# Two transformer blocks on one core: the first mixture of experts gathers for four experts and spreads for two, with rows over 32 handled in conditions; values of the second attention one step later

## The reference, cut to what matters

```python
logits = xt @ w_router + b_router
top_v, top_e = lax.top_k(logits, TOP_K)          # TOP_K = 4, N_EXPERTS = 32
weights = softmax(top_v)
hcat = x_pad[tok] @ w1[e] + b1[e]                # 1024 -> 2048
x_glu = minimum(hcat[:, ::2], 7.0)
x_lin = clip(hcat[:, 1::2], -7.0, 7.0)
act = x_glu * sigmoid(1.702 * x_glu) * (x_lin + 1.0)
y = act @ w2[e] + b2[e]                          # 1024 -> 1024
out = sum(y[dest] * weights)                     # over the token's 4 experts
```

## Time and profile before

| | us |
|---|---|
| median of 3 runs | 2189.37 |
| lowest, highest | 2186.71, 2189.53 |
| the profiled execution's own time | 2187.02 |
| its span | 2185.2 |
| mean granted TensorE clock | 0.927 of full |

### The profile page before, as it was taken

How to read it: one execution, slowest core, us unless ns; L and a number is a source line. 1 busy time by engine, 2 the same in 40 slices (tenths; PEclk the granted TensorE clock), 3 DMA queues, 4 the chain that set the end, 5 groups by cost and what they waited for, 6 DMA issues and landing times. The chain is left out here.

```text
span 2185.2 us, 28329 instructions
## 1 busy us (share of the span) xinstructions
PE 1818.3 (83%) x11496; PEld 826.7 (38%) x11496; DVE 804.7 (37%) x1613; ACT 506.8 (23%) x1028; POOL 77.5 (4%) x96
## 2 busy tenths in 40 slices
PE   7899998999999998989987797699889855665556
PEld 3655445433333433424333233255544522222221
DVE  2215533333342444434443334588782200000001
ACT  2022302232331233332333233222310200000000
POOL 0000000000000000000000000084000000000000
PEclk9999999999999999989999999799999878887888
DMA  7845359789897799999999999534128299999997
GB/s 281 287 136 191 136 173 388 314 350 409 343 420 312 309 424 423 423 422 399 425 423 423 422 423 423 180 121 178 54 101 345 87 429 427 427 428 428 427 429 322
DMA packets 114820, 713.55 MB, mean 327 GB/s; under 512 B 16799, under 2 KB 21102, under 8 KB 69006
## 3 DMA queue, kind: packets, MB, share of 16 engines
q1 hardware_dynamic: 106208, 704.98, 79.1%
q10 hardware_dynamic: 8398, 5.47, 0.8%
HBM read 709.35 MB, written 1.07 MB: 325 GB/s over the span
## 5 line engine op out<-in xcount | busy, mean ns | idle before, releaser
L881 PE MATMUL ps<-ring,ar 128*32 128x512 f32 x3072 | 371.9, 624 | 44.3 <-DMA ring<-in_w 31.6
L481 PE MATMUL ps<-ar 128*128 128x128 f32 (+5 forms) x1742 | 351.4, 359 | 38.3 <-PEq L755 16.4
L488 PE MATMUL ps<-ring,ar 128*32 128x512 f32 x1184 | 196.1, 692 | 139.0 <-DMA ring<-in_w_gate 49.2
L481 PEld LDWEIGHTS ps<-ar 128*128 128x128 f32 (+2 forms) x1742 | 233.9, 200 | 159.4 <-issue 114.3
L481 PE MATMUL ps<-ring,ar 128*128 128x512 f32 (+2 forms) x592 | 247.0, 577 | 4.9 <-ACT ar L2266 2.6
L881 PEld LDWEIGHTS ps<-ring,ar 128*32 128x32 f32 x3072 | 97.8, 113 | 314.3 <-issue 264.7
L1825 DVE TENSOR_SCALAR ar<-ps 128x256 f32<-128x256 f32 x128 | 54.4, 425 | 409.7 <-PE ps L881 400.9
L893 PE MATMUL ps<-ring,ar 128*32 128x512 f32 x1536 | 173.8, 598 | 0.0
L596 PE MATMUL ps<-ring,ar 128*128 128x512 f32 x384 | 171.9, 599 | 0.0
L481 PEld LDWEIGHTS ps<-ring,ar 128*128 128x128 f32 x592 | 112.4, 191 | 132.8 <-issue 126.2
L2400 ACT ACTIVATE ar<-ps 64x512 f32<-64x512 f32 x256 | 151.5, 592 | 45.1 <-PE ps L893 30.7
(11 more groups left out here) (403 smaller groups left out, 1379.0 us busy)
## 6 DMA issues: line engine op xcount, KB each, us to landing
ring<-in_w SPq DMA_DIRECT2D x192, 2048.0 KB, 20.4
ring<-in_w_gate SPq DMA_DIRECT2D x25, 2048.0 KB, 29.1
ring<-in_w_up SPq DMA_DIRECT2D x25, 2048.0 KB, 31.4
ring<-in_w_down SPq DMA_DIRECT2D x24, 2048.0 KB, 29.8
ring<-in_w_in SPq DMA_DIRECT2D x21, 2048.0 KB, 9.0
ring<-in_w_ada SPq DMA_DIRECT2D x12, 2048.0 KB, 8.3
ar<-in_w_up SPq DMA_DIRECT2D x7, 2048.0 KB, 29.8
ar<-in_w_gate SPq DMA_DIRECT2D x7, 2048.0 KB, 29.3
```

The costliest lines, as they stand in the source:

```text
L481: ins = self.t.e.matmul(o, l, r, start=(i == 0), stop=(i == len(pairs) - 1))
L488: ins = self.t.e.matmul(b[32 * i:32 * i + 32, :], l, r, start=(k == 0), stop=(k == len(steps) - 1))
L881: ins = e.matmul(b[32 * s:32 * s + 32, :], HG[:, 2 * c + r, 32 * n:32 * n + 32], W[:, r, HALF(s)], start=False, stop=(c == 3 and r == 1))
```

## The change

In the first mixture:
- The first 32 rows of four experts are gathered by one set of sixteen matmuls (32 columns each) into `HG4`, during the turn of expert 4g-1. The first four experts are split in two and two (`HEAD = 2`).
- Rows 33 to 128 are gathered for each expert in the condition on 32 rows, in the first half of its first layer, between pass 0 and the further passes, into `HGX` (96 columns). ACT copies them for every expert.
- The weights of the first 32 rows are turned for two experts together, and their spread (`spread_pair`, K = 128) runs once per two experts, during the turn of the even one. The weights of the further rows are turned and copied in the second layer, in the condition on 32.
- The spread of the further rows (`spread_further`) is in the condition on 32 (before: 64), with an inner condition on 96 per token block.
- YV is set to zero at the start and all spreads are added. Activations (`ATB`) and gathered further rows have one buffer instead of two.

In the second attention the values run one step later (15 steps instead of 14).

The second mixture's functions are only renamed. The diff, cut to its core:

```diff
-    HGB = [A(1024 * i, 8, 128) for i in range(2)]
-    ATB = [A(2048 + 1024 * i, 8, 128) for i in range(2)]
+    HG4, HGX, ATB, ACB = A(0, 8, 128), A(1024, 8, 96), A(1792, 8, 128), A(2816, 4, 256)
+    YGP, YGX, YG3 = A(3840, 1024), A(4864, 1024), A(HT, 1024, part=(64, 128))
...
+    HEAD = 2
...
+    def gather_four(t, w, g, lo, n):
+        t.wait_ge(s_dve, dve["pick4", g, lo])
+        t.wait_ge(s_act, act["rows", 1])
+        for h in range(2):
+            b = w.claim("hg", 1, g, lo, h, lane=TL1)
+            for k in range(4):
+                o = b[:, 128 * k + 32 * lo:128 * k + 32 * lo + 32 * n]
+                pe["hg", 1, g, lo, h, k] = w.sums(o, [(XNV[:, tb, TB(4 * h + k)], SB4[:, tb, 32 * lo:32 * lo + 32 * n])
+                                                     for tb in range(2)])
+
+    def turn_pair(t, w, j):
+        b = w.claim("swtp", j, lane=TL1)
+        t.wait_ge(s_dve, dve["selp", j])
+        for tb in range(2):
+            ins = t.e.transpose(b[:, TB(tb)], SWBP[:, tb, :], ident)
+        pe["swtp", j] = t(ins)
...
+    def spread_pair(t, w, j):
+        t.wait_ge(s_act, act["ygp", j])
+        for tb in range(2):
+            for h in range(2):
+                b = w.claim("spp", j, tb, h, lane=TL1)
+                pe["spp", j, tb, h] = w.sums(b[:, :], [(SWTP[:, TB(tb)], YGP[:, HALF(h)])])
...
+        def spread_further(u, count):
+            def further_rows():
+                t.wait_ge(s_act, act["ygx", u])
                 for tb in range(2):
+                    bs = [w.claim("spx", u, tb, h, lane=TL1X) for h in range(2)]
+                    k = z.n
+                    with e.If(count > 96):
...
+                    z.n = k
+                    with e.Else():
+                        for h in range(2):
+                            psp[u, tb, h] = z(e.matmul(bs[h][:, :], SWTX[:, TB(tb)], YGX[:, HALF(h)], start=True,
+                                                       stop=True))
+            either(t, z, count, 32, further_rows)
...
+                def gather_further():
+                    t.wait_ge(s_dve, dve["pickx", u])
+                    for h in range(2):
+                        for k in range(4):
+                            for tb in range(2):
+                                ins = e.matmul(hx[h][:, 96 * k:96 * k + 96], XNV[:, tb, TB(4 * h + k)],
+                                               SBX[u % 2][:, tb, :], start=(tb == 0), stop=(tb == 1))
+                        px["hx", u, h] = x(ins)
...
                 def second():
+                    if half == 0:
+                        gather_further()
+                    t.wait_ge(s_act, act["hx", u, half])
                     only(t, count, 64, third)
                     x(further(1))
...
             if u > 0:
-                spread1(u - 1, counts[u - 1])
+                spread_further(u - 1, counts[u - 1])
+            if u > 0 and u % 2 == 0:
+                spread_pair(t, w, u // 2 - 1)
...
             pe["at", u, 0] = t(turn_act(0, (0,)))
-            if u + 1 < NE:
-                gather(t, w, 1, u + 1, TL1)
+            if u == HEAD - 1:
+                gather_four(t, w, 0, HEAD, 4 - HEAD)
+            elif u % 4 == 3 and u + 1 < NE:
+                gather_four(t, w, u // 4 + 1, 0, 4)
+            if u > 0 and u % 2 == 0:
+                turn_pair(t, w, u // 2)
             turn_act(1, (1,))
+            at2, swx = w.claim("at", u, 2, lane=TL1), w.claim("swx", u, lane=TL1)
...
             with e.If(count > 32):
                 only(t, count, 64, lambda: turn_act(2, (2, 3)))
+                t.wait_ge(s_dve, dve["selx", u])
+                for tb in range(2):
+                    e.transpose(swx[:, TB(tb)], SWBX[:, tb, 0:128], ident)
+                    ins = e.transpose(swx[0:64, TB(2 + tb)], SWBX[:, tb, 128:192], ident)
+                px["swx", u] = x(ins)
...
-        for s in range(14):
+        for s in range(15):
             if s < 12:
                 scores(s)
-            if s >= 2:
+            if 2 <= s < 14:
                 turn_p(t, w, 2, s - 2, (0, 1), 2)
...
-            if s >= 2:
-                values(s - 2)
+            if s >= 3:
+                values(s - 3)
...
         vector_ada(v, 5, 1)
+        v(v.own.memset(YV, 0.0))
...
         for u in range(NE):
+            if u > 0 and u % 2 == 0:
+                vector_selectp(v, u // 2)
+            vector_selectx(v, u)
...
+            if u % 4 == 3 and u + 1 < NE:
+                vector_pick4(v, u // 4 + 1, 0, 4, RKP)
             if u + 1 < NE:
-                vector_pick(v, 1, u + 1)
-                vector_select(v, 1, u + 1)
+                vector_pickx(v, u + 1)
...
                 if n == 0 and u > 0:
-                    vector_spread(v, 1, u - 1)
+                    vector_spread_further(v, u - 1)
+                    if u % 2 == 0:
+                        vector_spread_pair(v, u // 2 - 1)
...
         for u in range(NE):
+            scalar_further(s, u)
             sigmoid(u, 0)
             turned_act(s, u, 0, (0,))
-            if u + 1 < NE:
-                scalar_gather(s, 1, u + 1, l1, lambda: sigmoid(u, 1))
+            if u == HEAD - 1:
+                scalar_four(s, 0, HEAD, 4 - HEAD, lambda: sigmoid(u, 1))
+            elif u % 4 == 3 and u + 1 < NE:
+                scalar_four(s, u // 4 + 1, 0, 4, lambda: sigmoid(u, 1))
             else:
                 sigmoid(u, 1)
+            if u > 0 and u % 2 == 0:
+                scalar_pair(s, u // 2)
             turned_act(s, u, 1, (1,))
...
-            evict(u, 0)
+            k = evict(u, 0)
+            if u % 2 == 1:
+                act["ygp", u // 2] = k
             turned_act(s, u, 2, (2, 3))
+            scalar_weights_further(s, u)
             for n in (1, 2, 3):
                 k = evict(u, n)
-                if n % 2:
-                    act["yg", 1, u, n // 2] = k
+            act["ygx", u] = k
...
-        for k in range(14):
-            if k >= 3:
-                values(k - 3)
-            if k >= 2:
+        for k in range(15):
+            if k >= 4:
+                values(k - 4)
+            if 2 <= k < 14:
                 scalar_turned_p(s, 2, k - 2, 4)
```

More of the change, by code:

```diff
@@ L1145, in tensor_moe2 @@
             if u > 0:
[L1146 removed]
+                spread(t, w, u - 1, TL2)
             if u + 1 < NE // 4:
[L1148 removed]
+                gather(t, w, u + 1, TL2)
             t.wait_ge(s_dve, dve["ac2", u])
@@ new lines, in vector_selectp @@
+    def vector_selectp(v, j):
+        if j > 0:
+            v.wait_ge(s_pe, pe["swtp", j - 1])
+        for x in range(2):
+            u = 2 * j + x
+            for tb in range(2):
+                k = v(v.own.tensor_scalar(SWBP[:, tb, 64 * x:64 * x + 64].rearrange("p (d s) -> p d s", d=2),
+                                          bc(SB4[:, tb, 32 * (u % 4):32 * (u % 4) + 32], 1, [128, 2, 32]),
+                                          (CMB if u < HEAD else CMBP)[:, tb, u:u + 1], None, ALU.mult))
+        dve["selp", j] = k
@@ new lines, in vector_pickx, with vector_selectx @@
+    def vector_pickx(v, u):
+        if u > 1:
+            v.wait_ge(s_px, px["hx", u - 2, 1])
+        dve["pickx", u] = v(v.own.tensor_tensor(
+            SBX[u % 2], bc(iota[:, 32:128], 1, [128, 2, 96]),
+            (RK if u < HEAD else RKP)[:, :, u:u + 1].to_broadcast([128, 2, 96]), ALU.is_equal))
+    def vector_selectx(v, u):
+        if u > 0:
+            v.wait_ge(s_px, px["swx", u - 1])
+        for tb in range(2):
+            twice = bc(SBX[u % 2][:, tb, :].rearrange("p (n s) -> p n s", n=3), 2, [128, 3, 2, 32])
+            k = v(v.own.tensor_scalar(SWBX[:, tb, :].rearrange("p (n d s) -> p n d s", n=3, d=2), twice,
+                                      (CMB if u < HEAD else CMBP)[:, tb, u:u + 1], None, ALU.mult))
+        dve["selx", u] = k
@@ L1752, in vector_spread @@
+    def vector_spread(v, u):
         order = [(tb, h) for tb in range(2) for h in range(2)]
-        if m == 2 and u == NE // 4 - 1:
+        if u == NE // 4 - 1:
             order = [(tb, h) for h in range(2) for tb in range(2)]
         for tb, h in order:
-            v.wait_ge(s_pe, pe["sp", m, u, 0, tb, h])
-            add(0, tb, h)
-        def second_half():
+            v.wait_ge(s_pe, pe["sp", 2, u, 0, tb, h])
+            o = XV[:, tb, HALF(h)]
+            dve["sum", 2, u, 0, tb, h] = v(v.own.tensor_tensor(o, ps("sp", 2, u, 0, tb, h)[:, :], o, ALU.add))
+            read["sp", 2, u, 0, tb, h] = v.mark()
@@ L1760, in second_half, with vector_spread_pair, vector_spread_further @@
+    def vector_spread_pair(v, j):
+        for tb in range(2):
+            for h in range(2):
+                v.wait_ge(s_pe, pe["spp", j, tb, h])
+                o = YV[:, tb, HALF(h)]
+                v(v.own.tensor_tensor(o, ps("spp", j, tb, h)[:, :], o, ALU.add))
+                read["spp", j, tb, h] = v.mark()
+    def vector_spread_further(v, u):
+        n, met = v.n, dict(v.met)
+        count = v.e.value_load(flag(u))
```

(1 more changed line is left out.)

266 lines of the change are left out of this document (133 added, 133 removed).

## The result

| | before | after |
|---|---|---|
| median of the runs, us | 2189.45 (2186.71 to 2191.01, 4 runs) | 2209.06 (2207.32 to 2220.17, 4 runs) |
| ratio, 95% interval | | 1.0102 [1.0067, 1.0136] |
| profiled execution, span and own time | 2185.2, 2187.02 | 2205.5, 2207.32 |
| mean granted clock over the span | 0.927 | 0.908 |
| first layer of expert 0 starts | 391.7 | 393.9 |

The change costs some 20 us (15 to 30 by the interval of the ratio). The range ended at 2205, so the time lies outside it. The lag grows at two places: 12 us from expert 0 to 9 (on top of 2 at the start) and 14 more behind them; the tail and the attention give some back.

A forecast was written before the change was run, and what follows sets the result against it. PE was taken to bound experts 0 to 9, expert 18 and the tail, DMA the other experts. Mixture +9.0, tail −5.4 and attention −7.0 gave −3.4 on the profiled 2187.0; forecast median 2186.0 us, range 2167 to 2205.

The forecast's parts named there:

- Which stage decides: First mixture: PE's work counts in experts 0 to 9, expert 18 and the tail; in the other 21 it moves slack.
- late spot: 1000 to 1020 us, expert 18: DMA falls to 0.87, some 2.8 us lost; there the change's +2.4 counts in full.
- Experts 0 to 9: First mixture up to expert 9's end, where PE sets the pace: the experts' terms sum to +6.6 us.
- +1.2 of expert 0: Expert 0: new gather +3.7, a shorter second layer (10.2 against 11.9), and 0.8 less before it.
- the 2.49 us: PE's idle time ahead of expert 1's spread; half assumed to stay, so experts 1 and 7 give −1.2 each.
- The steps inside an expert: Even experts with further rows: saved gather uncovers DVE, new gather costs 3.7 ahead of E; net +2.4 us each.
- E to T: From the end of an expert's first layer on PE to its second's: 20.0 us against 21.3 in even three-pass experts.
- The tail: Expert 31, end of the first mixture: no spread after its first layer, so the last spread starts earlier; −5.4 us.
- The attention: Second attention: values one step later end PE's waits for ScalarE's copy, DVE is next; −7.0 us.
- upper bound of 10.3: Second attention: largest gain from the later values, 11 steps at 0.94 us each.
- Rival C: PE's control and clock: 12.5 us for five skipped bodies, 8.5 for clock, giving +17.6, 2207 us; chance 0.27.
- the two prices: Cost of PE's new inner conditions: plain branches at about 108 ns, about 1 us for ten, or idle time like 2.49 us.

The follow-up runs named there:

- e10: Changed kernel with DVE's additions of the spreads moved behind the first three operations of the second pass; 2202.59 us, ratio 1.0066.
- e11: Changed kernel with DVE's additions of the spreads moved later, as in e10, and no code of the fourth pass (rows from 96 on); 2176.18 us, ratio 0.9944.
- e4: Changed kernel without the never-run code of the fourth pass (rows from 96 on) on PE in both layers; 2182.18 us, ratio 0.9973.
- e1: Kernel before with only the attention part of the change (values one step later); 2182.24 us, ratio 0.9975.
- e6: Kernel before without the never-run code of the fourth pass (rows from 96 on) on PE in both layers; 2180.78 us, ratio 0.997.
- e8: Kernel before with the attention part of the change and no code of the fourth pass (rows from 96 on); 2174.17 us, ratio 0.9944.
- e13: e8 with 16 never-run matmuls put into the condition of layer 1's first half; 2174.0 us, ratio 0.9936.

## Why the prediction was wrong

**Which stage decides: half right.** Up to expert 9 PE sets the pace, as said. The step that failed is the next: that in the 21 other experts the change "moves slack". That held for what PE executes, whose records fell by 28 us of busy time between expert 10 and 18. But the slack was 31.6 us of waits for weights, and the prediction's sum has no new wait for the sequencer and never asked how much slack was left. The runs showed in its place 40 us more of waits for instructions over all 32 experts, which brought the slack to 1.4. From expert 9's end to expert 31's first layer the lag grew by 14.1 us where +2.4 stood for expert 18. (The late spot that the prediction reads as 20 × 0.14 = 2.8 us is 2.6 by the 0.87 of the earlier trace rows; no term of the sum hangs on it.)

**Experts 0 to 9: +14.4 instead of +6.6.** What each expert adds to the lag, by the starts of the experts, after minus before:

| expert | start | 0 | 1 | 2 | 3 | 4 | 5 | 6 | 7 | 8 | 9 |
|---|---|---|---|---|---|---|---|---|---|---|---|
| predicted | | +1.2 | −1.2 | +2.4 | −2.4 | +2.4 | −1.6 | +2.4 | −1.2 | +2.4 | +2.2 |
| measured | +2.2 | +2.2 | +3.4 | +4.6 | −2.7 | +2.9 | 0.0 | +0.9 | −2.4 | +2.0 | +1.3 |

The predicted +1.2 of expert 0 held a gain of 0.8 ahead of it: the gather there took 7.09 us for its 32 records against 5.64, at a granted clock of 0.66 in 380 to 400 us against 0.83. Most of the rest is experts 1 and 2. Timeline of PE, after:

```profile
436.62 1.98 PE L867 MATMUL ps<-ar 128*128 128x512 f32 x4 [2.80 <-PEq L757]
439.75 1.98 PE L867 MATMUL ps<-ar 128*128 128x512 f32 x4 [1.15 <-DVE ar L1851]
...
453.24 1.93 PE L900 MATMUL ps<-ar 32*32 32x512 f32 x8 [3.61 <-PEq L1025]
455.10 5.34 PE L907 MATMUL ps<-ring,ar 128*32 128x512 f32 x32
460.36 3.81 PE L949 MATMUL ps<-ar 128*128 128x96 f32 x32
...
483.53 3.70 PE L483 MATMUL ps<-ar 128*128 128x512 f32 x8
...
490.26 0.41 PE L931 MATMUL ps<-ar 128*128 128x128 f32 x2 [2.60 <-DVE ar L1925]
490.60 3.64 PE L918 MATMUL ps<-ring,ar 128*32 128x512 f32 x32
...
503.42 1.06 PE L900 MATMUL ps<-ar 32*32 32x512 f32 x8
```

The wait of 3.61 us in front of expert 2 had no row before, and 5.34 instead of 3.64 us follows it: about 5 us at a place where the prediction had no term. The sequencer stands in front of the spread, as the 2.49 us did, and the prediction had halved that for experts 1 and 7.

**The steps inside an expert: right.** From 483.53 to 503.42 is 19.9 us, for E to T = 20.0; the transposes of pass 1 wait 2.60 us for DVE; the spread's second pair waits 1.15 for the adds; the gather of 96 columns takes 3.81 us, 0.1 more than taken. The statement that the saved gather uncovers DVE was right, and e10 and e11 price what the order of DVE adds to it: some 6 us, which the prediction had taken as given.

**The tail: right.** −6.5 for −5.4 (the lag falls from 28.5 to 22.0). The spread starts 12.1 us after the first layer's end, not 16.9. PE, after, beside the earlier trace rows:

```profile
1404.03 0.64 PE L931 MATMUL ps<-ar 128*128 128x128 f32 x2 [2.26 <-DVEq L1856]
1406.39 0.66 PE L931 MATMUL ps<-ar 128*128 128x128 f32 x2 [1.71 <-DVE ar L1925]
...
1413.87 3.76 PE L483 MATMUL ps<-ar 128*128 128x512 f32 x8 [1.34 <-ACT ar L2516]
```

**Between tail and attention** the lag grows again by 2.8 us, with no term in the prediction; e10 and e11 have 0.5 there and e4 3.0, so it isn't tied to the edits tried; its cause stays open.

**The attention: right in kind, 5.3 for 7.0.** L1120 (the former L1067) no longer waits for ScalarE, 0.4 us for 6.3, and DVE is next, at the turned weights. PE's waits from 1535 to 1590 us, after:

```profile
PE ps L615 <- DVE ar L1602: 2.7, 2, 1.8
PE ps L1120 <- ACT ar L2645: 0.4, 1, 0.4
```

These 2.7 us are about half of the 5 that lack to the upper bound of 10.3; DVE costs more here than the prediction took off for it.

**Rival C** came out, near its 2207, with 0.27 of chance. Its kind of wait, PE for its own sequencer, is the one that the runs show, but its places were wrong and its price was right by luck: it charged five bodies with 2.5 us and the clock with 8.5. In truth the waits for the sequencer grew by 40 us over all experts, most of them beside slack. Set against the kernels before that ran beside them, the parts are −5.3 for the attention (e1), +6 for DVE's order (e10 and e11), and +18 for code: the fourth pass costs the kernel after 25 us (e4) and the kernel before 7 (e6). That is 19, against 19.6 measured, and each part is uncertain by some us. The change adds only 5 packets itself; what it does more is to take executed work from PE, beside which the packets had come. That this is the larger share is argued, not shown. With neither the fourth pass nor the early additions, the new mixture (e11) and the old (e8) are level: fewer gathers and spreads gain nothing here, where PE's waits for DVE are 100 us against 21. Of the two prices that the prediction set side by side, a plain branch was the wrong one for these places: the waits are up to 4.9 us each, and they end with a packet.

## What to carry to other kernels

In all these kernels code behind a condition was loaded whether it ran or not: count the instructions of every body that most iterations skip, and look at the instruction queue's packets and at PE's waits for its own sequencer before adding to them; a new operation in a rarely taken branch may cost every iteration. In a stretch that DMA bounds, read how long PE waits for the weights: that is the slack; a change can use up all of it unseen, and then what is added counts. And when work is taken from the engine that sets the pace, look at once at what the next engine does in between, and let it do what the first waits for ahead of what nobody waits for.

## What was not expected of the hardware

- Sixteen matmuls per expert that never run cost 26 us in one place, 16 in another, and nothing in a kernel with 26 packets less (e8 against e13).
- Instruction packets of 16,384 bytes take 1.07 us each but seldom start less than 5.7 us apart, with weights streaming at 425 GB/s or not (from 391 to 740 us a tenth of the gaps is under 5.7 us after and 6.0 before).
- All 29 waits of PE of over 1 us for its sequencer, after, end 2.2 to 3.3 us behind the start of such a packet.
- A wait of PE costs twice: behind 3.56 us of idle time 32 records took 5.34 instead of 3.64 us, and over the stretch from expert 10 to 18 the granted clock was 0.91 against 0.94 before.
